# A tuned two-block transformer kernel: weight splits, attention steps and convolution steps issued in another order

## The reference

```
first_block:                                    # tokens 272 x 1024
    h = h + pool_mixer(rmsnorm(h))              # windows 2, 4, 8, 16
    h = h + swiglu(rmsnorm(h))                  # hidden 2816
    a = rmsnorm(h); q, k, v = a @ sb_w_qkv      # 16 heads of 64
    z = q k^T / 8                               # stick-breaking attention, strictly causal
    h = h + (exp(log_sigmoid(z) + sum of later log_sigmoid(-z)) @ v) @ sb_w_o
    h = h + swiglu(rmsnorm(h)); h = rmsnorm(h)[:, 16:]
second_block:                                   # tokens 256 x 1024, modulated by c
    q, k, v, hv, hx1, hx2, gna, ghy = h @ w_in
    y_na = neighbourhood attention(q, k, v) with 256 context keys and a bias, 8 heads of 64
    u = short_conv([hv, hx1, hx2])              # 3 taps
    filt = MLP with sines, times a decay        # 2 filters, forward and backward
    y_hy = two gated long convolutions of u with filt (by FFT)
    x = x + g1 * gated_merge(...); x = x + g2 * swiglu(...); return rmsnorm(x)
```

## Time and profile before

| | before |
|---|---|
| median of 3 runs | 1008.97 us (1008.65 to 1009.53) |
| the profiled execution's own time | 1008.65 us |
| its span (first to last instruction) | 1006.9 us |
| PE, DVE, ACT busy | 989.8, 789.5, 556.4 us |
| attention rounds on PE | about 241 to 350 us of the span |
| mix stage on PE | about 574 to 760 us |
| granted TensorE clock, mean | 0.996 of full speed |

### The profile page before, as it was taken

How to read it: one execution, slowest core, us unless ns; L and a number is a source line. 1 busy time by engine, 2 the same in 40 slices (tenths; PEclk the granted TensorE clock), 3 DMA queues, 4 the chain that set the end, 5 groups by cost and what they waited for, 6 DMA issues and landing times.

```text
span 1006.9 us, 19808 instructions
## 1 busy us (share of the span) xinstructions
PE 989.8 (98%) x7928; PEld 960.1 (95%) x7928; DVE 789.5 (78%) x1409; ACT 556.4 (55%) x931; POOL 22.3 (2%) x28
## 2 busy tenths in 40 slices
PE   9999999999999999999999999999999999999996
PEld 6999999999889999999999999998899999999996
DVE  5888889975899878989887676789986786766543
ACT  5654444443777665555454548795644565454442
POOL 4000000000000000000000000000001100000000
PEclk9999999999999999999999999999999999999998
DMA  8666667884443248987677414355335556565541
GB/s 301 220 206 225 210 213 254 287 313 131 144 131 125 90 143 309 316 272 228 220 268 248 152 43 137 100 149 187 105 108 166 179 183 200 173 192 171 167 141 42
DMA packets 53573, 187.49 MB, mean 186 GB/s; under 512 B 6120, under 2 KB 7689, under 8 KB 53034
## 3 DMA queue, kind: packets, MB, share of 16 engines
q1 hardware_dynamic: 53306, 185.64, 55.6%
q10 hardware_dynamic: 176, 0.59, 0.2%
HBM read 185.16 MB, written 1.05 MB: 185 GB/s over the span
## 4 chain that ended last, share of the span: by engine, by line
PE 78%; DVE 15%; ACT 4%; issue 2%; DMA 0%; DVEq 0%; POOL 0%; ACTq 0%; POOLq 0%
PE psum L441 77%; DVE memr L994 5%; DVE memr L1016 3%; ACT memr L1684 1%; DVE memr L1200 1%; DVE mem L1197 1%; PE psum L456 1%; DVE mem L1191 1%; ACT mem L1695 1%; ACT memr L1695 1%; DMA mem<-in_w_up 0%; ACT mem L1826 0%; DVE mem L1157 0%; DVE psum L1182 0%; DVE psum L1438 0%
## 5 line engine op out<-in xcount | busy, mean ns | idle before, releaser
L441 PE MATMUL psum<-memr 128*128 128x256 f32 (+5 forms) x7652 | 953.7, 287 | 3.7 <-DVE memr L1016 1.9
L441 PEld LDWEIGHTS psum<-memr 128*128 128x128 f32 (+1 forms) x7652 | 928.2, 188 | 22.7 <-issue 7.1
L994 DVE TENSOR_TENSOR memr<-mem,memr 128x1024 fp32r<-128x1024 f32 (+1 forms) x290 | 337.3, 1200 | 57.9 <-ACT memr L1684 57.5
L1684 ACT ACTIVATE memr<-mem 128x1024 fp32r<-128x1024 f32 (+2 forms) x296 | 290.6, 1025 | 20.9 <-PE psum L441 8.9
L1695 ACT ACTIVATE memr<-mem 128x256 fp32r<-128x256 f32 (+4 forms) x171 | 81.5, 484 | 276.7 <-DVE mem L1126 103.3
L1016 DVE TENSOR_TENSOR memr<-mem,memr 128x256 fp32r<-128x256 f32 (+2 forms) x129 | 61.5, 485 | 9.1 <-ACT memr L1695 7.9
L1111 DVE TENSOR_TENSOR mem<-psum,mem 128x256 f32<-128x256 f32 (+1 forms) x66 | 28.0, 424 | 43.8 <-PE psum L441 43.8
L1004 DVE CUSTOM_DVE_ANT_0 mem<-mem 128x1024 f32<-128x1024 f32 x48 | 58.6, 1220 | 0.6
L1692 ACT ACTIVATE mem<-mem 128x256 f32<-128x256 f32 (+1 forms) x56 | 22.8, 413 | 65.2 <-DVE mem L1651 31.9
L1016 DVE TENSOR_TENSOR memr<-psum,memr 128x256 fp32r<-128x256 f32 (+2 forms) x72 | 32.2, 463 | 13.3 <-ACT memr L1695 12.5
L1695 ACT ACTIVATE memr<-psum 128x256 fp32r<-128x256 f32 (+3 forms) x80 | 29.6, 405 | 7.7 <-PE psum L456 4.0
(11 more groups left out here) (131 smaller groups left out, 385.1 us busy)
## 6 DMA issues: line engine op xcount, KB each, us to landing
mem<-in_w_gate SPq DMA_DIRECT2D x66, 512.0 KB, 4.0
mem<-in_w_up SPq DMA_DIRECT2D x66, 512.0 KB, 4.4
mem<-in_w_ada SPq DMA_DIRECT2D x48, 512.0 KB, 4.5
mem<-in_w_down SPq DMA_DIRECT2D x48, 448.0 KB, 4.5
mem<-in_w_in SPq DMA_DIRECT2D x40, 512.0 KB, 4.5
mem<-in_w_down SPq DMA_DIRECT2D x24, 512.0 KB, 4.8
mem<-in_sb_qkv SPq DMA_DIRECT2D x24, 512.0 KB, 4.6
mem<-in_sb_o SPq DMA_DIRECT2D x8, 512.0 KB, 3.2
```

Of the source, the lines that this page charges most:

```text
L441: return pe.matmul(out, a, b, start=start, stop=stop)
L994: dve.tensor_tensor(r(ol, n), raw(e), rf(oh, n), ALU.subtract).then_inc(w_lo, 1)
L1684: act.activation(r(oh, n), raw(e), ACT.Copy).then_inc(w_hi, 1)
```

## The change

Only the order of steps is changed, in seven places; no instruction is added or taken away.

- In the attention, the second round (j = 2) gets the form of the later ones. On PE, `attend(0)` moves from behind the value product to ahead of `v_turn(1)`. ACT and DVE split three weight tiles (up to `W_SB + 12`) before the round, then one each where the later rounds do it. `out_low(0)` and `out_high(0)` move up likewise.
- In the mix stage, `h_rows(3)` moves on PE from behind `na_turn(3)` to ahead of `g_mm(4)`, and `h_rows(5)` from behind `g_mm(6)` to ahead of `h_mm(7)`.
- On DVE and ACT, the weight splits (`used`) go to other places, `na_low(2)` goes ahead of `softmax(3)`, `na_low(3)`, `used(14)` and `h_conv(5)`, `used(15)` ahead of the filter tile, `matrix_low(1)` behind `used(22)`, and `matrix_high(1)` behind `used(22)` and `spectrum(1)`.
- SP loads one weight tile more before the filter's weights.

```diff
--- before.py
+++ after.py
@@ -653,12 +653,9 @@
             if j == 2:
                 turn(0)
             qkv(j, "k")
-            if j > 2:
-                attend(j - 2)
+            attend(j - 2)
             v_turn(j - 1)
             qkv(j, "v")
-            if j == 2:
-                attend(0)
             turn(j - 1)
         scores(7)
         sbo(0, 0, 6)
@@ -869,9 +866,9 @@
         h_rows(2)
         h_mm(3)
         h_mm(4)
+        h_rows(3)
         g_mm(4)
         na_turn(3)
-        h_rows(3)
         g_mm(5)
         h_rows(4)
         na_attend(3)
@@ -881,9 +878,9 @@
         pe.wait_ge(table_lo, 1)
         filter_tile(0)
         h_mm(6)
+        h_rows(5)
         h_mm(7)
         g_mm(6)
-        h_rows(5)
         pe.wait_ge(table_lo, 2)
         spectrum(0)
         filter_tile(1)
@@ -1230,25 +1227,23 @@
         qk_low(1)
         chain(0)
         v_low(0)
+        low_halves(W_SB + 12)
         for j in range(2, KT):
             if j > 2:
                 turned_low(j - 2)
             q_out(j)
-            low_halves(W_SB + (3 * j + 7 if j > 2 else 10))
+            low_halves(W_SB + 3 * j + 7)
             masks(j - 1)
             if j == 2:
                 turned_low(0)
             chain(j - 1)
             k_out(j)
             if j < KT - 1:
-                low_halves(W_SB + (3 * j + 8 if j > 2 else 12))
-            if j > 2:
-                out_low(j - 2)
+                low_halves(W_SB + 3 * j + 8)
+            out_low(j - 2)
             qk_low(j)
             v_low(j - 1)
             low_halves(W_SB + 3 * j + 9)
-            if j == 2:
-                out_low(0)
         turned_low(6)
         masks(7)
         chain(7)
@@ -1499,23 +1494,24 @@
         used(6)
         h_conv(2)
         weights_low(2)
+        used(7)
         q_step(3)
         q_turned(3)
-        used(8)
+        used(9)
+        na_low(2)
         softmax(3)
-        na_low(2)
         softmax_sums(3)
-        used(9)
         u_low(2)
         h_conv(3)
         used(10)
         h_conv(4)
-        used(12)
         weights_low(3)
         u_low(3)
         dve.wait_ge(table_hi, 1)
         minus(r(W3S, 2048, 64, 128), f(W3R, 2048, 0, 64), rf(W3S, 2048, 0, 64)).then_inc(table_lo, 1)
         used(13)
+        na_low(3)
+        used(14)
 
 
         def matrix_low(n):
@@ -1571,11 +1567,9 @@
                     minus(r(o + 2048, 512), x, rf(o, 512)).then_inc(dt_dve, 1)
 
         matrix_low(0)
-        used(14)
-        na_low(3)
-        filter_tile(0)
         h_conv(5)
         used(15)
+        filter_tile(0)
         h_conv(6)
         h_conv(7)
         used(18)
@@ -1587,8 +1581,8 @@
             dve.scalar_tensor_tensor(hx(i, NMETA, T1), hx(i, NMETA, T1), vec("final_norm", i), f(SROOT, T1),
                                      ALU.mult, ALU.mult)
         h_conv(10)
+        used(22)
         matrix_low(1)
-        used(22)
         h_conv(11)
         used(23)
         transform(0)
@@ -1857,25 +1851,22 @@
         k_high(1)
         sticks(0)
         v_high(0)
+        high_halves(W_SB + 12)
         v_copy(1)
         for j in range(2, KT):
             if j > 2:
                 turned_high(j - 2)
-                high_halves(W_SB + 3 * j + 7)
+            high_halves(W_SB + 3 * j + 7)
             q_high(j)
             if j == 2:
-                high_halves(W_SB + 10)
                 turned_high(0)
             sticks(j - 1)
-            high_halves(W_SB + (3 * j + 8 if j > 2 else 12))
-            if j > 2:
-                out_high(j - 2)
+            high_halves(W_SB + 3 * j + 8)
+            out_high(j - 2)
             k_high(j)
             v_high(j - 1)
             high_halves(W_SB + 3 * j + 9)
             v_copy(j)
-            if j == 2:
-                out_high(0)
         turned_high(6)
         sticks(7)
         v_high(7)
@@ -2102,25 +2093,28 @@
         h_step(2)
         gate(2)
         weights_high(2)
+        used(7)
         q_step(3)
         q_turned(3)
         gate(3)
-        used(8)
+        used(9)
         na_high(2)
-        used(9)
         softmax(3)
         softmax_scale(3)
         h_rows(2)
         h_step(3)
         used(10)
         h_step(4)
-        used(12)
-        gate(4)
         weights_high(3)
         h_rows(3)
         act.wait_ge(w3_in, 16)
         copy(r(W3S, 2048, 0, 64), f(W3R, 2048, 0, 64)).then_inc(table_hi, 1)
+        gate(4)
         used(13)
+        gate(5)
+        h_rows(4)
+        na_high(3)
+        used(14)
 
 
         def matrix_high(n):
@@ -2155,17 +2149,13 @@
                     copy(r(YB + 1024 * i + 512 * ft, 512), f(base[i], 512)).then_inc(y_hi, 1)
 
         matrix_high(0)
-        gate(5)
-        used(14)
-        h_rows(4)
-        na_high(3)
         h_step(5)
+        used(15)
         filter_high(0, 0)
-        used(15)
         h_step(6)
+        h_rows(5)
         used(16)
         filter_high(0, 1)
-        h_rows(5)
         h_step(7)
         used(17)
         gate(6)
@@ -2181,8 +2171,8 @@
         h_step(10)
         early_gates()
         used(22)
+        spectrum(1)
         matrix_high(1)
-        spectrum(1)
         h_step(11)
         used(23)
         transform(0)
@@ -2313,7 +2303,7 @@
             sp.wait_ge(ns_least, 4 * p + 4)
             bias(2 * p + 2)
             bias(2 * p + 3)
-        raws(W_MIX + 19)
+        raws(W_MIX + 20)
         sp.wait_ge(ns_mm, 8)
         sp.wait_ge(ns_least, 16)
         sp.dma_start(f(W3R, 2048, 0, 64), T["hy_w3"]).then_inc(w3_in, 16)
```

## The result

| | before | after |
|---|---|---|
| median, same chip | 1009.24 us (4 runs) | 1019.89 us (4 runs, 1016.61 to 1020.13) |
| ratio | | 1.0099, 95% interval 1.0078 to 1.0119 |
| the profiled execution's own time, its span | 1008.65, 1006.9 us | 1019.51, 1017.7 us |
| granted TensorE clock, mean | 0.996 | 0.991 |

The changed kernel is slower by 10.65 us, about 1%. The forecast was 1015.8 us, 7.15 us more than the profiled execution; the measured time lies 4.1 us above the forecast, 0.1 us above the upper end of the wide range (1010.5 to 1019.8) and well above the forecast's own range (1013 to 1018). The direction and the stalls came as worked out. The clock took several times what it was given.

The account below looks back on a forecast made before the run. PE, busy 989.8 of 1006.9 us, bounds the kernel, so its waits are paid in full. 1008.65 + 6.15 for waits + 1.0 for the clock = 1015.8 us; own range 1013 to 1018, wide range 1010.5 to 1019.8.

Parts of the forecast that it names:

- The clock: Half clock behind the 4.3 us mix-stage stall at h_rows(3): 0 to 4.65 us more, taken as 1.0 us.
- DVE 1.6 us ahead in the attention: Attention: DVE's new order starts turned_low(1) 1.6 us earlier, and the stage ends 1.6 us earlier; bounds 0 and 2.8.
- for the 3.3 us stall I count nothing: Attention: no clock loss was counted for PE's 3.3 us stall at attend(0), 70 us ahead of where DVE decides.
- The chain of the mix stage: Mix stage: softmax(3) 2.0 us later, h_rows(3) waits 4.3, DVE's filter half 2.75 later, 4.4 more work; spectrum(0) 6.0 later.
- the forecast's two tile splits: Mix stage, DVE: two more tiles to split ahead of the filter tile, 2.27 us, part of its 4.4 us of added work.
- The matrices: Mix stage's end: matrix_low(1) and matrix_high(1) move back, transform(0) starts 1.9 us later; price 1.75 us, bounds 0 and 1.9.
- if ACT had slack: Mix stage's end: condition under which moving the matrix steps on ACT and DVE would cost 0 us.
- The sum of the waits: Whole kernel: -1.6 for the attention, +6.0 for the spectrum, +1.75 for the transform, together +6.15 us.
- the clock falls and stays low: Rival: clock falls at both stalls and holds through the work behind; mix +4.65, attention gains 1 less; 1020.4 us, chance 0.12.
- Half the chain: Rival, mix stage: ACT passes on none of PE's lateness, filter tile later by 4.4 us alone; 1011.5 us, chance 0.12.
- Faster: Rival: the 2.23 us convolution wait goes, nothing replaces it, and the attention gives 1.6; 1004.8 us, chance 0.06.
- The attention does not make its stall good: Rival, attention: the 1.6 us gain is lost and the 3.3 us stall is paid; 1020.7 us, chance 0.04.

Follow-up runs that it names:

- experiment 1: The changed kernel with products of two constants put on PE ahead of its four long waits: 1014.42 us, ratio 1.0057 to the kernel before.
- experiment 7: Changed kernel with h_rows(3), tile 1 matrices and filter-tile order (with h_rows(5)) put back, dummy products ahead of attend(0) and h_rows(5): 1009.0 us, 1.0004 to before.
- experiment 2: Two kernels against the one before: all mix-stage and SP edits without the attention's, 1020.46 us (1.012); the attention edits alone, 1008.32 us (0.9998).
- experiment 4: The changed kernel with h_rows(3) put back behind na_turn(3) on PE: 1012.69 us, ratio 1.0039 to the kernel before.
- experiment 5: The changed kernel with matrix_low(1) back ahead of used(22) and matrix_high(1) ahead of spectrum(1): 1016.54 us, ratio 1.0073 to the kernel before.

## Why the prediction was right, and where it was off

- **DVE 1.6 us ahead in the attention: right** (1.45 us at `turned_low(1)`), and so was the 3.3 us stall of `attend(0)` (3.28). That the stage would end 1.6 us earlier held at full clock (-1.52, experiment 1), and in the changed kernel only by 0.58 us. The step "for the 3.3 us stall I count nothing: it lies 70 us ahead of the place where DVE decides" failed: the forecast had PE at the last scores 0.3 us ahead of DVE (0.56 at full clock, experiment 1), and half clock behind the stall took 1.5: those 0.56 and 0.94 of the lead. The 70 us were no cover, since PE ran through every round on the way without a wait in which to make the loss good.
- **The chain of the mix stage: right, step by step.** `softmax(3)` and `h_conv(3)` were 2.0 and 1.9 us late against the stage's start, as forecast, and `h_rows(3)` waited 4.53 us (4.3). At full clock DVE began its half of the filter's weights 2.76 us later (2.75), the spectrum shifted by 6.02 us (6.0) and the transform by 7.97 (7.75); `h_rows(5)` did not wait. From the end of that half to the end of the filter tile DVE took 17.4 us, 13.0 before: 4.5 us more (4.4). Taken back one after the other, the edits return 3.1 us for `h_rows(3)`, 0.9 for the filter tile's place and 2.0 for the splits and copies. The last agrees with the 2.27 us of the forecast's two tile splits by luck alone: in experiment 7 the spectrum does not wait for DVE, and the 2.0 us are the small waits on PE, of which the forecast had one.
- **The matrices: right in size.** A wait of 2.01 us (1.9). The forecast put it down to ACT; the rows show DVE late by the same amount through its own two splits, and the forecast's bound of 0, "if ACT had slack", would not have been reached.
- **The sum of the waits:** +6.15 forecast; with the clock held +5.6 by the medians, and 7.97 - 1.52 = +6.45 by the rows. The spans of the two profiled executions differ by 5.5 us only. Of that gap to the rows 0.65 us is that the one with the dummy products reached the key product earlier (at 256.84, before at 257.49), ahead of everything that was changed.
- **The clock: the term that was mis-sized.** It was given 1.0 us and took 4.2 to 5.5 (experiment 1). The mechanism named for it was wrong too: not one fall of unknown length at the longest stall, but one of 3.41 us behind each of four waits, also those of 2.6 and 2.0 us, which the forecast had as waits and not as clock. The evidence that it leaned on, the full clock behind the 2.23 us gap, was one draw: in experiment 2 the clock fell behind this gap. This term is why the median lies above the forecast's own range; only the wide range, which was opened toward the clock's case, comes near it.
- **The rival "the clock falls and stays low"** gave 1020.4 us, which is near the measured 1019.9, for another reason: its 4.65 us at `h_rows(3)` was 1.4 us there (4.25 for 3.06 and 0.66 for 0.44), and the rest came from places where it had none.
- **The other rivals fell.** *Half the chain* had ACT pass none of PE's lateness on, and ACT passed on as much as forecast (the 2.76 us above). *Faster* needed `h_conv(3)` by 663.3, and it was the wait of 4.53 us. *The attention does not make its stall good* needed later last scores, and they came 0.58 us earlier.

The Trainium skill ("TensorE: Matmul & The Clock Gate", section "Why this matters for your kernels") warns of idle gaps between bursts of matmuls, and the forecast weighed it against the earlier trace rows and followed the row. The page was the better guide for the two long stalls, though in one profile (experiment 2) the stall of 3.29 us had no fall. For the 2.6 and 2.0 us waits only the runs here tell.

## What to carry to other kernels

When an engine with a gated clock gets a new wait, price the wait and, beside it, the work behind it at half clock: here up to 1.7 us behind each of the four waits of 2 us or more in the changed kernel (and 2.4 to 2.6 in the two profiles where a fall lasted 6.82 us, against the same steps at full clock), which nearly doubled the loss. A single profile with a full clock behind a gap does not show that the gap is free, so look at several. And where a wait can't be removed, products of constants ahead of it are a cheap test of how much of its cost is the clock, and sometimes a remedy.

## What the runs showed of the hardware

- Each fall to half clock ahead of the kernel's end lasted 3.41 us, but for one in experiment 4 and one in experiment 5, which lasted 6.82.
- Behind the same wait the fall comes in some executions only. Over all the profiles, with the waits not filled: `h_rows(3)` (4.5 us) 3 falls in 3 profiles, `attend(0)` (3.3 us) 3 in 4, the spectrum (2.6 us) 4 in 4, `h_rows(5)` (2.2 us) 1 in 3, the transform (2.0 us) 2 in 3. The wait of 1.1 to 1.2 us at the last scores had none in 5. The one fall that follows shorter waits is that at the kernel's end, of which the forecast speaks: 1.12 us, eight one-column products, and 0.96 us more.
- Products of constants of 128 columns, which left at most 0.8 us of a wait unfilled, held the clock at 1.00: behind the 12 waits that were filled so, in six profiles, it did not fall once.
